# Tile 3's first normalisation on ScalarE and GpSimd instead of VectorE, in a fused decoder layer

## What is computed

```python
x = layer_norm(DN_ALPHA * x + merged @ w_out[l], ln1_g[l], ln1_b[l])
moe = grouped_moe(x, w_router, b_router, w_gate, w_up, w_down)
x = layer_norm(DN_ALPHA * x + moe, ln2_g[l], ln2_b[l])
```

## Time and profile before

| | us |
|---|---|
| median of 3 runs | 841.67 |
| lowest, highest | 841.57, 844.1 |
| profiled execution | 843.93 |
| its span, first to last instruction | 842.3 |

### The profile page before, as it was taken

The page is one execution under the profiler, slowest core; times in us unless marked ns, Lnnn a source line. Parts: engine busy times, 40 slices in busy tenths (PEclk is TensorE's granted clock), DMA queues, the critical chain, the costliest instruction groups (busy, mean ns, idle before and its releaser), DMA issues.

```text
span 842.3 us, 11117 instructions
## 1 busy us (share of the span) xinstructions
PE 823.0 (98%) x3825; PEld 681.3 (81%) x3825; DVE 572.6 (68%) x658; ACT 449.1 (53%) x455; POOL 73.6 (9%) x74
## 2 busy tenths in 40 slices
PE   9999999999999999999999999999999999999984
PEld 9888888888888888888888888887888888888752
DVE  4877444434458985422555688979998889998548
ACT  4655523434566663423242334668788787887620
POOL 1000000100000000000000000732011111010140
PEclk9999999999999999999999999999999999999997
DMA  6332334553333333335423835899999999999552
GB/s 203 93 112 86 101 95 150 188 167 100 100 89 99 88 99 101 98 101 153 135 87 129 320 112 213 241 377 404 395 395 386 389 394 378 387 382 390 200 216 100
DMA packets 112338, 173.76 MB, mean 206 GB/s; under 512 B 7455, under 2 KB 90056, under 8 KB 100534
## 3 DMA queue, kind: packets, MB, share of 16 engines
q1 hardware_dynamic: 106342, 159.80, 53.5%
q0 software_dynamic: 5968, 13.61, 4.4%
HBM read 163.49 MB, written 16.82 MB: 214 GB/s over the span
## 4 chain that ended last, share of the span: by engine, by line
PE 89%; DVE 4%; issue 2%; POOL 2%; DMA 1%; ACT 1%; DVEq 0%; ACTq 0%; POOLq 0%
PE psA L654 8%; PE psA L656 8%; PE psA L655 8%; PE psB L654 6%; PE psB L655 6%; PE psB L656 6%; PE psA L841 6%; PE psA L843 6%; PE psA L842 5%; PE psB L866 3%; PE psB L868 3%; PE psB L867 3%; PE psD L655 2%; PE psD L654 2%; PE psC L655 2%
## 5 line engine op out<-in xcount | busy, mean ns | idle before, releaser
L1498 DVE TENSOR_TENSOR elo<-est,ehi 128x2048 fp32r<-128x2048 f32 x96 | 215.1, 2287 | 31.0 <-ACT ehi L1132 30.4
L1132 ACT ACTIVATE ehi<-est 128x2048 fp32r<-128x2048 f32 x96 | 180.3, 1915 | 28.8 <-DMA est<-in_w_exp_down_dram 15.3
L1288 DVE TENSOR_TENSOR wlo<-wst,whi 128x1024 fp32r<-128x1024 f32 (+1 forms) x76 | 95.1, 1251 | 85.4 <-ACT whi L963 84.4
L963 ACT ACTIVATE whi<-wst 128x1024 fp32r<-128x1024 f32 (+1 forms) x76 | 81.9, 1077 | 75.9 <-PE psB L656 30.7
L841 PE MATMUL psA<-ehi,xe_hi 128*128 128x512 f32 x256 | 101.4, 396 | 0.9 <-DVE xe_lo L1717 0.5
L843 PE MATMUL psA<-ehi,xe_lo 128*128 128x512 f32 x256 | 99.9, 390 | 0.0
L842 PE MATMUL psA<-elo,xe_hi 128*128 128x512 f32 x256 | 99.7, 389 | 0.0
L654 PE MATMUL psB<-xT_hi,whi 128*128 128x512 f32 x208 | 81.0, 390 | 0.0
L656 PE MATMUL psB<-xT_hi,wlo 128*128 128x512 f32 x208 | 80.9, 389 | 0.0
L655 PE MATMUL psB<-xT_lo,whi 128*128 128x512 f32 x208 | 80.9, 389 | 0.0
L841 PEld LDWEIGHTS psA<-ehi,xe_hi 128*128 128x128 f32 x256 | 48.2, 188 | 10.7 <-issue 1.3
(11 more groups left out here) (331 smaller groups left out, 1503.8 us busy)
## 6 DMA issues: line engine op xcount, KB each, us to landing
est<-in_w_exp_gate_dram SPq DMA_DIRECT2D x32, 1024.0 KB, 12.4
est<-in_w_exp_up_dram SPq DMA_DIRECT2D x32, 1024.0 KB, 10.9
est<-in_w_exp_down_dram SPq DMA_DIRECT2D x32, 1024.0 KB, 12.2
wst<-in_w_in_dram SPq DMA_DIRECT2D x60, 512.0 KB, 3.9
wst<-in_w_branch_r_dram SPq DMA_DIRECT2D x8, 640.0 KB, 4.4
ys<-zero POOLq DMA_DIRECT2D x8, 512.0 KB, 2.9
wst<-in_w_branch_a_dram SPq DMA_DIRECT2D x8, 512.0 KB, 3.5
o_st<-in_w_out_dram SPq DMA_DIRECT2D x8, 512.0 KB, 4.5
```

Of the source, the lines that this page charges most:

```text
L963: A(whi[p][:, 0:K, :], wst[p][:, 0:K, :], ACT.Copy).then_inc(w_hi, 1)
L1132: A(ehi[s][:], est[s][:], ACT.Copy).then_inc(gu_hi if s < 4 else d_hi, 1)
L1288: V.tensor_tensor(wlo[p][:, 0:K, :], wst[p][:, 0:K, :], whi[p][:, 0:K, :], ALU.subtract).then_inc(w_lo, 1)
L1498: V.tensor_tensor(elo[s][:], est[s][:], ehi[s][:], ALU.subtract).then_inc(gu_lo if s < 4 else d_lo, 1)
```

## The change

Tile 3's two halves are no longer normalised on VectorE. VectorE writes minus mean times scale into `st1[:, 3, 0:1]` (one instruction on one column, right after the one that releases the Exp). ScalarE, after the Exp, multiplies each half by the scale and adds that offset (Identity with both as per-partition operands). GpSimd multiplies each half by g and adds b, in two `tensor_tensor` passes, and its second pass of a half raises `x1_half` or `x1_done`. VectorE's calls of `spread_half` go away.

```diff
+            for h in range(2):
+                row = x1[:, TT - 1, h * S:(h + 1) * S]
+                pool.wait_ge(scaled, h + 1)
+                nc.gpsimd.tensor_tensor(row, row, ln1_gb[0][:, h * S:(h + 1) * S], ALU.mult).then_inc(gained, 1)
+                pool.wait_ge(gained, h + 1)
+                nc.gpsimd.tensor_tensor(row, row, ln1_gb[1][:, h * S:(h + 1) * S],
+                                        ALU.add).then_inc((x1_half, x1_done)[h], 1)
+
             pool.wait_ge(x1_stored, 16 * TT)
...
             A(r16[1][:], r16[0][:], ACT.Exp).then_inc(exp_done, 1)
+            act.wait_ge(shift_done, 1)
+            for h in range(2):
+                row = x1[:, TT - 1, h * S:(h + 1) * S]
+                A(row, row, ACT.Identity, bias=st1[:, TT - 1, 0:1], scale=st1[:, TT - 1, 18:19]).then_inc(scaled, 1)
             act.wait_ge(o_done, HALVES * TT)
...
             V.tensor_tensor(r16[0][:], lb[:], b16(r1[0][:]), ALU.subtract).then_inc(lmax_done, 1)
+            V.tensor_scalar(st1[:, TT - 1, 0:1], st1[:, TT - 1, 19:20], -1.0, None, ALU.mult).then_inc(shift_done, 1)
             beats(won_e, fours(lb))
...
-            spread_half(TT - 1, 0, x1_half)
             dve.wait_ge(pos_done, 1)
...
-            spread_half(TT - 1, 1, x1_done)
             listed(1)
```

More of the change, by code:

```diff
@@ L281, in trunk_moe @@
         x1_half = sem("x1_half")
+        shift_done = sem("shift_done")
+        scaled = sem("scaled")
+        gained = sem("gained")
         folding = sem("folding")
@@ L1528, in spread @@
                                        ALU.mult, ALU.add).then_inc(x1_done, 1)
[L1530 to L1537, removed]
             def moments(halves, u):
```

## The result

The changed kernel takes 846.94 us (median of 10 runs, 844.4 to 850.09) where the kernel before takes 842.44 (10 runs beside them, 841.26 to 844.1). The ratio is 1.005, with a 95% interval of 1.0034 to 1.0066. The profiled execution has a span of 848.0 us, 5.7 more than before.

A forecast was written before the change was run, and what follows sets the result against it. TensorE was taken to bound the kernel. The gather's 4.0 us delay under the lock plus 1.7 for the clock made 5.7 us, so 841.67 + 5.7 = 847.4 us; own range 844.0 to 849.1, 8 in 10 range 841.0 to 848.6.

The forecast's parts named there:

- What bounds the kernel: TensorE, 98% busy and 89% of the chain; a shift of its start into expert 0 reaches the end nearly whole.
- The stage: TensorE from the start of its 14 fillers to expert 0's first product, the stretch where the forecast put its loss.
- What was removed: Four VectorE passes, 3.0 us together; only TensorE's 0.55 us wait for `first_by` can go, then its fillers are late next.
- The added instructions: VectorE's one-column instruction 0.1 us on the router's chain; ScalarE's two passes cost nothing; GpSimd passes 1.2 us each.
- The lock: In the router, GpSimd passes and VectorE instructions with two SBUF inputs exclude each other both ways; gather 4.0 us later.
- The side that no row of before could show: VectorE's two-SBUF-input instruction standing still behind a GpSimd pass; earlier rows showed only GpSimd waiting for VectorE.
- The rule of the Trainium skill: A two-SBUF-input VectorE instruction and a GpSimd instruction reading SBUF exclude each other; whichever issues second waits.
- The rival without hindrance: GpSimd and VectorE don't hinder each other, or only GpSimd waits; `sel` by 511.7, time 841.2 us, chance 0.34.
- Its size: Gather start 4.0 us later under full alternation in the router, 2.3 us in the milder order.
- the order of turns: VectorE's router comparisons and GpSimd's four passes alternate, one comparison between two passes; `sel` at 516.0 in place of 511.45.
- The clock: TensorE, idle before the position matmuls, drops to 1.2 GHz: 1.7 us lost, bounds 0 and 3.4.

The follow-up runs named there:

- experiment 3: Changed kernel and changed kernel with 32 TensorE fillers in place of 14, both repeated on one chip: 847.24 and 847.21 us against 842.56 for the kernel before.
- experiment 2: Changed kernel with 32 fillers in place of 14 on TensorE ahead of the position matmuls: 846.46 us against 842.75 for the kernel before, ratio 1.0039.
- experiment 4: Kernel before plus four GpSimd multiplications of 128x512 into a scratch buffer nobody reads: 846.43 us against 842.75, ratio 1.0041.
- experiment 5: Kernel before plus six GpSimd memsets of 128x1024 into a scratch buffer: 843.43 us against 842.75, ratio 1.0003.
- experiment 1: Changed kernel with GpSimd's four passes started only after `sel` is written: 843.63 us against 842.75 for the kernel before, ratio 1.0014.

## Why the prediction was right

*What bounds the kernel.* Right in the main. The stage's 5.7 us stand in the span, too, but the exact match is luck: the parts ahead of and behind the stage differ by 0.57 and 0.58 us in opposite directions. In the repetition (experiment 3) the stage is 5.4 us longer and the span only 3.5. The medians moved by 4.5 and 4.7, so most of the stage's loss reaches the end; whether later waits take up the rest, or these stages were longer than usual, isn't shown.

*What was removed.* Right. The wait of 0.55 for `first_by` is gone, and the fillers became last. At full clock (experiment 2) the gather starts 517.28 - 515.39 = 1.9 us behind `sel`, 2.05 in the forecast.

*The added instructions.* Right within 0.1 us. ScalarE's two passes took 1.50 us together (1.56 forecast), no table load came, and `x1_half` and `x1_done` never were last. GpSimd's first pass began 2.62 us behind the mark, where the forecast had 509.7 - 507.13 = 2.57. A pass took 1.29 to 1.30, not 1.2: by 1.29 for 512 columns and 2.36 for 1024 about 0.2 us of it is fixed.

*The lock.* The side that no row of before could show is shown: by the ends of the four long instructions, and in isolation by experiments 4 and 5. The rule of the Trainium skill (SBUF — State Buffer, section "Who interferes with whom") held in the direction that decides here. For the other one, GpSimd behind VectorE, the runs add nothing to the earlier trace rows: GpSimd's passes over 512 columns took 1.26 to 1.36 us in every run, whatever VectorE had to do. The rival without hindrance, to which I gave 0.34, would have had `sel` end by 511.7; aligned at the fillers it ended at 515.1.

*Its size.* Forecast 4.0 us for the gather, measured 3.0 at full clock. The step that was too large is the order of turns. I let one comparison through between two passes, so all four passes lay ahead of the last comparisons and `sel`. In fact two went through between the second and third pass and the other four around the start of the fourth, and `sel` waited for the fourth pass only in part: `sel` was 3.7 us late, not 4.55.

*The clock.* Forecast 1.7 us; in the profiled execution 11.94 us from `sel` to expert 0 against 524.52 - 515.39 = 9.13 with fillers, so 2.8 us. It ran low for some 6 us, longer than behind the waits of the earlier trace rows. The two errors, 1.0 too much and 1.1 too little, cancel: 5.7 forecast, 5.7 in this execution. The median moved by less, 4.5 and in the repetition 4.7, and 846.94 lies below the 847.4 of the forecast, inside its range; it is as near as that also because the forecast started from 841.67, where the kernel before measured 842.44 beside it. That the clock is a term of its own in the median, I could not show.

*What the working lacked.* It named only two-input instructions as exposed. The single-input `first_by` and L1638 are exposed too (experiments 1, 4 and 5). In the changed kernel this cost nothing, because GpSimd was done (514.46) before `first_by` began (515.54). With the passes behind the router it cost 0.8 us of the gather, and the wait for `x1_half` ahead of it another 0.5; neither had I foreseen.

## What to carry to other kernels

Before moving elementwise work from VectorE to GpSimd, list what VectorE runs at that time: each of its instructions with two SBUF inputs can wait for a whole GpSimd pass, so a chain of 0.2 us instructions grows by up to a pass at every one. TENSOR_SCALARs with one SBUF input belong on the list, too. Put GpSimd's passes where VectorE's instructions are off the path, or cut them short; moving to ScalarE had no such price. And look at what the relieved engine's work really delays: here 3.0 us were taken off VectorE for at most 0.55 us that TensorE waited for.

## What the runs showed of the hardware

- A VectorE TENSOR_SCALAR with one SBUF tensor input (128x64 fp32 with constants; 128x128 bf16 to fp32 with one value per partition) waits even for a GpSimd memset, which reads nothing: 0.38 us for 0.20, and 1.55 for 0.87 in four. The two-input TENSOR_TENSOR beside it doesn't (0.22). The 128x4 TENSOR_SCALARs of the keys waited for copies (1.23 us) but not for memsets (0.39); why is open.
- When both have work that excludes the other's, VectorE gets in after every single GpSimd instruction (its comparisons start 0.41 us apart beside GpSimd pieces of 128 columns, which start 0.42 apart). With passes over 512 columns, two comparisons got in between the second and the third pass and four between the third and the fourth.
- A GpSimd `tensor_tensor` in fp32 took 0.45 us for 128 columns (one starting every 0.42), 1.29 for 512 and 2.36 for 1024.
